# Small triangles in blocks of 32 on four row groups, and head pairs side by side

## The reference, cut to what matters

```python
# FoX: 4 heads of 64; c is the running sum of log_f over the tokens
s = einsum('qd,kd->qk', q, k) * scale + c[q] - c[k]     # causal, softmax, times v
# MoBA: 4 heads, here plain causal attention over 256 keys
# RWKV-7: 8 heads of 64, a recurrence over the 256 tokens
state = state * w + (state @ -kk)[:, None] * (kk * a)[None, :] + v[:, None] * k[None, :]
y = state @ r
```

## Time and profile before

| | before |
|---|---|
| median of 3 runs | 1879.29 us (1876.02 to 1880.2) |
| the profiled execution's own time | 1879.87 us |
| its span, first to last instruction | 1878.6 us |
| PE busy | 1840.2 us, 98% |
| VectorE busy | 1172.0 us, 62% |
| ScalarE busy | 928.5 us, 49% |
| GpSimd busy | 93.6 us, 5% |
| mean granted TensorE clock | 0.990 |
| mixer's part with the change, layer 0 | about 262 to 380 us |
| the same, layer 1 | about 922 to 1037 us |

### The profile page before, as it was taken

How to read it: one execution, slowest core, us unless ns; L and a number is a source line. 1 busy time by engine, 2 the same in 40 slices (tenths; PEclk the granted TensorE clock), 3 DMA queues, 4 the chain that set the end, 5 groups by cost and what they waited for, 6 DMA issues and landing times.

```text
span 1878.6 us, 27992 instructions
## 1 busy us (share of the span) xinstructions
PE 1840.2 (98%) x11596; PEld 1546.9 (82%) x11596; DVE 1172.0 (62%) x1653; ACT 928.5 (49%) x1413; POOL 93.6 (5%) x59
## 2 busy tenths in 40 slices
PE   7999999999999999999999999999999999999999
PEld 6888788878888888887888888888888888888887
DVE  5555577766655565555777666555688548697556
ACT  5444664234544454446642345444555654556553
POOL 0000010040000000000100400000010000000000
PEclk9999998999999999999999999999999999999999
DMA  6755442023455557554420235655554456554454
GB/s 239 249 189 179 168 146 68 25 80 113 158 190 189 191 173 249 191 189 159 156 68 25 80 112 170 207 189 190 167 167 158 156 193 203 168 171 159 159 186 140
DMA packets 83615, 299.18 MB, mean 159 GB/s; under 512 B 9632, under 2 KB 10784, under 8 KB 83232
## 3 DMA queue, kind: packets, MB, share of 16 engines
q1 hardware_dynamic: 79328, 287.87, 46.4%
q10 hardware_dynamic: 3840, 8.03, 1.2%
q0 software_dynamic: 320, 1.48, 0.2%
HBM read 296.30 MB, written 1.05 MB: 158 GB/s over the span
## 4 chain that ended last, share of the span: by engine, by line
PE 94%; DVE 4%; ACT 1%; issue 1%; DMA 0%; POOL 0%; ACTq 0%; DVEq 0%
PE ps L343 24%; PE ps L345 24%; PE ps L344 24%; PE ps L361 2%; PE ps L362 2%; PE ps L363 2%; PE ps L799 1%; PE ps L1194 1%; PE ps L559 1%; PE ps L1197 1%; DVE wlo L325 1%; PE ps L398 1%; PE ps L1185 1%; PE ps L1597 1%; PE ps L771 1%
## 5 line engine op out<-in xcount | busy, mean ns | idle before, releaser
L325 DVE TENSOR_TENSOR wlo<-raw,whi 128x1024 fp32r<-128x1024 f32 (+1 forms) x546 | 662.7, 1222 | 397.2 <-ACT whi L316 395.9
L316 ACT ACTIVATE whi<-raw 128x1024 fp32r<-128x1024 f32 (+1 forms) x546 | 572.1, 1053 | 487.7 <-PE ps L345 460.6
L343 PE MATMUL ps<-whi,a_hi 128*128 128x512 f32 x1696 | 675.4, 398 | 6.7 <-DVE a_lo L1886 1.7
L345 PE MATMUL ps<-whi,a_lo 128*128 128x512 f32 x1696 | 662.3, 390 | 0.0
L344 PE MATMUL ps<-wlo,a_hi 128*128 128x512 f32 x1696 | 661.3, 390 | 0.0
L343 PEld LDWEIGHTS ps<-whi,a_hi 128*128 128x128 f32 x1696 | 319.1, 188 | 76.3 <-DVE a_lo L1886 2.2
L345 PEld LDWEIGHTS ps<-whi,a_lo 128*128 128x128 f32 x1696 | 318.8, 188 | 68.3
L344 PEld LDWEIGHTS ps<-wlo,a_hi 128*128 128x128 f32 x1696 | 319.4, 188 | 62.2
L343 PE MATMUL ps<-whi,h_hi 128*128 128x512 f32 x320 | 124.9, 390 | 0.0
L345 PE MATMUL ps<-whi,h_lo 128*128 128x512 f32 x320 | 124.6, 389 | 0.0
L344 PE MATMUL ps<-wlo,h_hi 128*128 128x512 f32 x320 | 124.5, 389 | 0.0
(11 more groups left out here) (317 smaller groups left out, 1792.9 us busy)
## 6 DMA issues: line engine op xcount, KB each, us to landing
raw<-stream SPq DMA_DIRECT2D x546, 512.0 KB, 3.4
arena<-rows ACTq DMA_DIRECT2D x2, 1026.0 KB, 13.4
arena<-mem ACTq DMA_DIRECT2D x2, 1024.0 KB, 9.7
arena<-lora ACTq DMA_DIRECT2D x2, 768.0 KB, 6.8
arena<-rows ACTq DMA_DIRECT2D x2, 512.0 KB, 4.4
const_tables<-consts POOLq DMA_DIRECT2D x1, 901.0 KB, 4.8
arena<-band POOLq DMA_DIRECT2D x1, 544.0 KB, 4.1
x_res<-x SPq DMA_DIRECT2D x1, 512.0 KB, 3.7
```

The lines of the kernel that those rows point to most:

```text
L316: self.split_hi.mark(act.activation(self.weights(self.whi, u), self.weights(self.raw, u), ACT.Copy), u)
L325: self.split_lo.mark(dve.tensor_tensor(self.weights(self.wlo, u), self.weights(self.raw, u), self.weights(self.whi, u).bitcast(F32), ALU.s ...
L343: pe.matmul(out, a_h, hi, start=start, stop=False, skip_group_check=True)
L345: last = pe.matmul(out, a_l, hi, start=False, stop=True, skip_group_check=True)
```

## The change

Three things change in the mixer of the first block.

1. The triangles are inverted by their diagonal blocks of 32 first. A group now has 4 heads x 4 blocks (`TRIANGLES`: block b on row group b and column group b), 32 x 32 x 32 each, up to level 4; T and its transpose are 32 columns wide per head, both start from PE (`pe_rw_inv0` now makes the triangle and its transpose, 256 records), and VectorE's work has half the columns. The last step (`pe_rw_last`) joins two blocks of 32 to one of 64 with 32 matmuls twice, on two diagonal tiles at a time. ScalarE copies T's blocks to `TI` (`act_rw_last`) and writes half of the joining blocks (`act_rw_last_out`); VectorE writes the other half (`dve_rw_last`).
2. The chunks' products are ordered so that an even and an odd head and the two chunks follow each other, and are marked by pairs of heads instead of heads.
3. FoX's logarithms are summed once, as rows (`pe_at_logs`, copied by `act_at_logs` to `CR`). The scores are made for four heads behind each other, and then one matmul with a single row is added for each head.

```diff
-    for lv in range(6):
+    i, j = s % 32, np.arange(32)[None, :]
+    c["eye32"] = i == j
+    c["pairs"] = np.concatenate([(i // 2 == j // 2) & (i < j), (i // 2 == j // 2) & (i > j)], 1)
+    for lv in range(1, 5):
         b = 1 << lv
         c[f"low{lv}"] = ((i // (2 * b)) == (j // (2 * b))) & ((i // b) % 2 == 1) & ((j // b) % 2 == 0)
-    c["lowT0"] = ((i // 2) == (j // 2)) & (i % 2 == 0) & (j % 2 == 1)
+    c["upper"] = (s // 32) % 2 == 0
...
-        self.T2 = [[t2[:, 512 * (2 * t + g):512 * (2 * t + g + 1)].rearrange("p (a h c) -> p a h c", a=2, h=4)
-                    for g in range(2)] for t in range(NT)]
-        self.XG = [[xn[:, 1024 + 256 * (2 * t + g):1280 + 256 * (2 * t + g)].rearrange("p (h c) -> p h c", h=4)
+
+        self.TC = [t2[:, 512 * t:512 * (t + 1)].rearrange("p (g a h c) -> p g a h c", g=2, a=2, h=4) for t in range(NT)]
+        self.TI = [t2[:, 1024 + 512 * t:1536 + 512 * t].rearrange("p (g h c) -> p g h c", g=2, h=4) for t in range(NT)]
+        self.XG = [[xn[:, 1024 + 128 * (2 * t + g):1152 + 128 * (2 * t + g)].rearrange("p (h c) -> p h c", h=4)
                     for g in range(2)] for t in range(NT)]
...
-        for n in part:
-            h0 = (0, 1, 4, 5)[n]
-            po = HD * (h0 % 2)
+        for pair in range(part[0] // 2, part[-1] // 2 + 1):
             if t:
-                pe.wait_ge(*self.rw_dve("masked", l, 0, n))
+                for n in (2 * pair, 2 * pair + 1):
+                    pe.wait_ge(*self.rw_dve("masked", l, 0, n))
             for i in range(2):
-                for c in range(2):
-                    cols = slice(t * P + c * HD, t * P + (c + 1) * HD)
-                    for a in range(2):
-                        ins = pe.matmul(self.bank(4 + n)[c * HD:(c + 1) * HD, i * 256 + a * P:i * 256 + (a + 1) * P],
-                                        self.BK[po:po + HD, a, h0 // 2 + i, cols],
-                                        self.AR[po:po + HD, 0:2, h0 // 2 + i, cols],
-                                        start=True, stop=True, skip_group_check=True)
-            m.mark(ins, "products", l, t, n)
+                for a in range(2):
+                    for c in range(2):
+                        cols = slice(t * P + c * HD, t * P + (c + 1) * HD)
+                        for odd in range(2):
+                            po = HD * odd
+                            ins = pe.matmul(self.bank(4 + 2 * pair + odd)[c * HD:(c + 1) * HD,
+                                                                          i * 256 + a * P:i * 256 + (a + 1) * P],
+                                            self.BK[po:po + HD, a, 2 * pair + i, cols],
+                                            self.AR[po:po + HD, 0:2, 2 * pair + i, cols],
+                                            start=True, stop=True, skip_group_check=True)
+            m.mark(ins, "products", l, t, pair)
 
     def dve_rw_products(self, l, t, part):
         dve = self.nc.vector
         mask = self.c("mask4").unsqueeze(1).to_broadcast([P, 2, 256])
         for n in part:
...
-        return self.bank(4 + 2 * t + g, 4 * HD).rearrange("p (h c) -> p h c", h=4)
+        return self.bank(4 + 2 * t + g, 128).rearrange("p (h c) -> p h c", h=4)
 
     def t4(self, t, g):
-        return self.bank(4 + 2 * t + g)[:, 4 * HD:8 * HD].rearrange("p (h c) -> p h c", h=4)
-
-    def b4(self, n):
-        return self.c(n).unsqueeze(1).to_broadcast([P, 4, HD])
+        return self.bank(4 + 2 * t + g)[:, 128:256].rearrange("p (h c) -> p h c", h=4)
+
+    def last4(self, t):
+        return self.bank(4 + 2 * t, 256).rearrange("p (g h c) -> p g h c", g=2, h=4)
 
     def pe_rw_inv0(self, l):
+
         pe = self.nc.tensor
         for t, g in self.GROUPS4:
             pe.wait_ge(*self.rw_dve("masked", l, 1, 2 * t + g))
+            A, B = (x[HD * g:HD * (g + 1), 0] for x in (self.AR, self.BK))
             for i in range(4):
-                for c in range(2):
-                    cols = slice(t * P + c * HD, t * P + (c + 1) * HD)
-                    ins = pe.matmul(self.x4(t, g)[c * HD:(c + 1) * HD, i, :], self.AR[HD * g:HD * (g + 1), 0, i, cols],
-                                    self.BK[HD * g:HD * (g + 1), 0, i, cols], start=True, stop=True, skip_group_check=True)
+                for b in range(4):
+                    rows, cols = slice(32 * b, 32 * b + 32), slice(t * P + 32 * b, t * P + 32 * b + 32)
+                    pe.matmul(self.x4(t, g)[rows, i, :], B[:, i, cols], A[:, i, cols], start=True, stop=True,
+                              skip_group_check=True)
+                for b in range(4):
+                    rows, cols = slice(32 * b, 32 * b + 32), slice(t * P + 32 * b, t * P + 32 * b + 32)
+                    ins = pe.matmul(self.t4(t, g)[rows, i, :], A[:, i, cols], B[:, i, cols], start=True, stop=True,
+                                    skip_group_check=True)
             self.rw_pe.mark(ins, "inv0", l, t, g)
 
     def dve_rw_inv0(self, l, groups):
         dve, m = self.nc.vector, self.rw_dve
+        pairs = self.c("pairs").rearrange("p (a c) -> p a c", a=2).unsqueeze(2).to_broadcast([P, 2, 4, 32])
+        eye = self.c("eye32").unsqueeze(1).to_broadcast([P, 8, 32])
         for t, g in groups:
-            T = self.T2[t][g]
...
-            eye = self.c("ident64").unsqueeze(1).to_broadcast([P, 8, HD])
+            ps = self.bank(4 + 2 * t + g, 256).rearrange("p (a h c) -> p a h c", a=2, h=4)
+            m.mark(dve.tensor_tensor(T, ps, pairs, ALU.mult), "pairs", l, t, g)
             T = T.rearrange("p a h c -> p (a h) c")
-            dve.wait_ge(*m("TI 0", l, t, g))
+            dve.wait_ge(*m("pairs", l, t, g))
             m.mark(dve.tensor_tensor(T, T, eye, ALU.add), "T", l, t, g, 0)
 
     def pe_rw_level(self, l, lv):
         pe, m = self.nc.tensor, self.rw_pe
         for t, g in self.GROUPS4:
+            T = self.TC[t][:, g]
             pe.wait_ge(*self.rw_dve("T", l, t, g, lv - 1))
             for i in range(4):
-                for c in range(2):
-                    co = slice(c * HD, (c + 1) * HD)
-                    ins = pe.matmul(self.x4(t, g)[co, i, :], self.MK[co, t, 2 * i + g, 0, :], self.T2[t][g][co, 1, i, :],
+                for rows, cols in self.TRIANGLES:
+                    ins = pe.matmul(self.x4(t, g)[rows, i, :], self.MK[rows, t, 2 * i + g, 0, cols], T[rows, 1, i, :],
                                     start=True, stop=True, skip_group_check=True)
             m.mark(ins, "level x", l, t, g, lv)
         for t, g in self.GROUPS4:
-            T, X = self.T2[t][g], self.XG[t][g]
+            T, X = self.TC[t][:, g], self.XG[t][g]
             pe.wait_ge(*self.rw_dve("X", l, t, g, lv))
             for i in range(4):
-                for c in range(2):
-                    co = slice(c * HD, (c + 1) * HD)
-                    ins = pe.matmul(self.x4(t, g)[co, i, :], X[co, i, :], T[co, 0, i, :], start=True, stop=True,
+                for rows, cols in self.TRIANGLES:
+                    pe.matmul(self.x4(t, g)[rows, i, :], X[rows, i, :], T[rows, 0, i, :], start=True, stop=True,
+                              skip_group_check=True)
+                for rows, cols in self.TRIANGLES:
+                    ins = pe.matmul(self.t4(t, g)[rows, i, :], T[rows, 0, i, :], X[rows, i, :], start=True, stop=True,
                                     skip_group_check=True)
-                    if lv < 5:
-                        ins = pe.matmul(self.t4(t, g)[co, i, :], T[co, 0, i, :], X[co, i, :], start=True, stop=True,
-                                        skip_group_check=True)
             m.mark(ins, "level", l, t, g, lv)
 
     def dve_rw_level(self, l, lv):
         dve, m = self.nc.vector, self.rw_dve
+        low = self.c(f"low{lv}").unsqueeze(1).to_broadcast([P, 4, 32])
         for t, g in self.GROUPS4:
             dve.wait_ge(*self.rw_pe("level x", l, t, g, lv))
-            m.mark(dve.tensor_tensor(self.XG[t][g], self.x4(t, g), self.b4(f"low{lv}"), ALU.mult), "X", l, t, g, lv)
+            m.mark(dve.tensor_tensor(self.XG[t][g], self.x4(t, g), low, ALU.mult), "X", l, t, g, lv)
         for t, g in self.GROUPS4:
-            n = 2 if lv < 5 else 1
-            T = self.T2[t][g][:, 0:n].rearrange("p a h c -> p (a h c)")
+            T = self.TC[t][:, g].rearrange("p a h c -> p (a h c)")
             dve.wait_ge(*self.rw_pe("level", l, t, g, lv))
-            m.mark(dve.tensor_tensor(T, T, self.bank(4 + 2 * t + g, 256 * n), ALU.add), "T", l, t, g, lv)
+            m.mark(dve.tensor_tensor(T, T, self.bank(4 + 2 * t + g, 256), ALU.add), "T", l, t, g, lv)
+
+    def pe_rw_last(self, l):
+
+        pe, m = self.nc.tensor, self.rw_pe
+        for t, g in self.GROUPS4:
+            pe.wait_ge(*self.rw_dve("T", l, t, g, 4))
+            for i in range(4):
+                for up, down in self.HALVES:
+                    ins = pe.matmul(self.x4(t, g)[down, i, :], self.MK[up, t, 2 * i + g, 0, 32:HD],
```

(99 more changed lines are left out.)

4 lines of the change are left out of this document (removed).

## The result

The kernel after takes 1911.03 us (median of 4 runs, 1904.13 to 1912.31) against 1879.04 us of the kernel before on the same chip (4 runs): ratio 1.0166, 95% interval 1.0149 to 1.0184. It is slower by 32 us, where I forecast 29 us less.

The account below looks back on a forecast made before the run. PE was taken as the bound, busy 1840 of 1878.6 us. Triangles 23.6 plus FoX 8.8 less clock 2.4 gave 30.0 us off the profiled 1879.87: 1850 us, with 8 in 10 between 1837 and 1876.

Parts of the forecast that it names:

- Can PE issue a weight load and a matmul each 7.9 ns?: Triangle levels: a burst of nine instructions in at most 20 ns made 7.9 ns a record likely, not certain.
- Rival 1: PE's issue bounds the triangles: no record sooner than 29.2 ns after the last, 1922 us in all; chance 12%.
- Rival 3: Triangle levels run at the lower clock, 8 us a layer and 16 in all, giving 1866 us; chance 12%.
- A record of 32x32: Triangle start and levels to 4: with four tiles, one record ends each 7.9 ns, each tile held 31.6 ns.
- The last step: Last triangle level, two tiles at a time: x and level 1.0 us each, 1.7 us saved a layer.
- my sum of 26.7 + 5: Time a 32x32 record holds its tile: 26.7 ns of streaming and 5 more, 31.6 ns.
- The wait for the masks: PE's wait for VectorE's masks of the products, before the triangles' start: from 1.7 to about 3.5 us.
- FoX: Scores by pairs and logarithms as rows in both layers: saves 8.8 us together.
- the 5.4 forecast: FoX in layer 0: saves 5.4 us, assuming the clock falls again at the second scores and returns earlier.
- forecast 3.4 better: FoX in layer 1, at full clock: scores save 1.4 + 3.45 us, the new logs cost 1.45, so 3.4 saved.
- Clock: Behind the longer wait for the masks: one more half-speed stretch of 3.4 us in both layers together, charged 2.4 us.
- The triangles as a whole: All triangle steps, from products through the last level: save 11.8 us a layer, 23.6 in two.

Follow-up runs that it names:

- the split matmuls: The kernel before, with each matmul of levels 1 to 4 made as two of 32 columns on its 64x64 tile: 1928.52 us, ratio 1.0255.

## Why the prediction was wrong

**The step that failed** is the one under "The triangles" that begins "Can PE issue a weight load and a matmul each 7.9 ns?". The answer was yes, and the question too small. The burst of the earlier trace rows shows nine instructions that were already at hand, and it says nothing of how fast new ones come. I counted a level as 384 records of 7.9 ns, 3.1 us. It is also 768 instructions, three blocks, and at 3.47 us a block at least 10.4 us. From the start of level to level measured 10.7 and 11.9 us for levels 1 to 3 (332.43, 343.09, 354.96), where I had 4.9 and 5.5 and the kernel before 7.0 and 7.3.

**What the kernel before could have told.** A level there is 384 instructions in 7.0 us, 4.7 us a block; in its densest run, x and level without a break, a block is 128 records of 29.2 ns, 3.74 us. It ran just above the supply's 3.47. All my rates were at that edge, so the trace of before could not show the limit, but the count of instructions against packets of q8 was there to be read.

**Rival 1** came nearest, "PE's issue is the bound", 12%, at 1922, against 1911 measured: its threshold (about 15.5 ns a record, 18 with FoX) held, as far as one case can say: the sustained rate is 27, and the change lost. Its mechanism was not right. The limit isn't the time from one record to the next, which went down to 8 ns, but a block of 256; and it lets short stretches pass, as the last level shows. **Rival 3** ("the levels run at the lower clock", 12%) came true as well, beside it: its sign, 0.50 from 333 us on, is there, from 332.10 to 355.99. I had priced it at 16 us for levels that are paced by PE's records; here they are mostly paced by the blocks.

**The other terms.** (1) A record of 32x32 each 7.9 ns forecast, from a tile that is held for 31.6 ns. Both came out at full clock in the first 32 records or so of a row, behind the first four: the starts are 7, 7, 6 and 12 ns apart, so the fourth waits for a tile, and four take 32 ns. The last step, with two tiles at a time, says the same, 64 records in 1.01 us, 15.8 ns each:

```profile
384.82 1.10 PE L1234 MATMUL ps<-arena 32*32 32x32 f32 x58
...
385.83 1.11 PE L1241 MATMUL ps<-arena 32*32 32x32 f32 x59
```

Later in a row the starts alternate, 15 and 2 ns, 8.5 a record; bf16 records come each 8.2 ns at either level of the clock. That is rather PE's own pace of starting a record, but no run separates it. What my sum of 26.7 + 5 doesn't explain is the rest: on 64x64 tiles the weights alone hold the tile as long as 64 columns do, and at the lower clock an fp32 record takes 13.3 ns, 53.3 a tile, which is 2 x 32 columns at 1.2 GHz with nothing on top. (2) The last step: 1.0 us each for x and level forecast, 1.01 and 1.04 measured. (3) The wait for the masks: "3 us or more", 3.1. (4) FoX: 8.8 forecast, 7.9 measured alone. How it divides between the layers one profile can't say, for the clock at the second scores is not the same from one profile to the next. Before, it fell there in layer 0 and not in layer 1, and I built both terms on that. In the profile of FoX's part alone it falls in both layers: layer 0 gave the 5.4 forecast (products at 308.62), layer 1, forecast 3.4 better, was 1.5 worse at its products:

```profile
934.09 2.08 PE L1613 MATMUL ps<-arena 64*128 64x256 f32 x8
936.10 2.08 PE L1617 MATMUL ps<-arena,const_tables 1*128 1x256 f32 x8
938.11 3.68 PE L1021 MATMUL ps<-const_tables,small 128*64 128x128 f32 x32
```

But FoX's change isn't needed for either. Two kernels have FoX's part as before. In the one with the triangles alone the clock does not fall at layer 0's second scores (first two rows, full clock) and the products begin at 306.41, sooner than with FoX's change; in the one with the split matmuls it does fall at layer 1's (last two rows):

```profile
276.39 0.70 PE L1652 MATMUL ps<-arena 64*128 64x256 f32 x2
282.29 1.97 PE L1022 MATMUL ps<-const_tables,small 128*64 128x128 f32 x32
...
967.52 1.22 PE L1598 MATMUL ps<-arena 64*128 64x256 f32 x2
972.97 3.26 PE L1019 MATMUL ps<-const_tables,small 128*64 128x128 f32 x28
```

So that the 5.4 of layer 0 came out is in part luck. Where neither profile has the fall in layer 1 (before, and FoX with the products' order), the way from layer 0's first right-hand side to layer 1's products took 587.5 and 584.3 us, 3.3 less, near the 3.4 forecast. In FoX's part alone 2.6 us came back in the triangles of layer 1, whose low stretch was shorter. (5) Clock, 2.4 forecast: the low stretches grew by 72 us, but mostly inside the levels that wait for instructions anyway. With 37 us of them less and the same instructions the time fell by 2 us, by about 8 at the very most, and blocks come each 3.47 us at either level, so the clock isn't the main cause. (6) The triangles as a whole: 11.8 a layer forecast; with bf16 operands the stage is 11.7 and 10.6 us shorter than before. That agrees, but flatters: half the records went too, and the steps from level to level were 5.6 and 7.4 us, not 4.9 and 5.5. What fp32 would take with instructions always at hand lies, as an estimate from these runs, between 1853 and 1886 (3584 records at 13.3 ns in place of 1792 at 8.2, all of them on PE's path), and no run shows it. So it isn't shown that the triangles would win even then.

Of the miss of 61 us (1850 to 1911), 7 lie between the profiled execution and the median. Of the other 54, 38.5 are the stops of the two layers read from the profile; the rest, some 16, I put down to what runs between stops, at 13.3 ns a record at the lower clock in place of 8, and the GEMM units behind the levels, which start at that clock (0.63 us for a matmul that takes 0.39). How these two divide I haven't separated, nor shown that they are all of it.

**What is best of what was run** with full precision: FoX's part alone, with the products' order, or with the last level by blocks besides, all 1872, 0.3 to 0.6% below the kernel before, with the 64x64 triangles kept.

## What to carry to other kernels

Small matmuls cost instructions before they cost array time: count PE's instructions in a stage (in this case four to an fp32 matmul, two to one with bf16 operands), divide by 256, and hold it against 3.5 us a block; if the planned work of a stage is shorter, the supply is the bound and array packing only adds to it. In a profile the sign is a stop of PE put down to issue at each 256th instruction, and packets of the instruction queue in step with it. A stretch of up to a block behind long matmuls ran free here (256 instructions in the last level, 346 to 506 behind the kernel), so packing can pay there, or where it doesn't raise the count.

## What the runs showed that I had not expected

- PE's instructions come in blocks of 256 (16 KB), one in 3.47 us at best, 13.6 ns an instruction, whether or not other engines transfer. After long matmuls 346 to 506 were ready at once; then each block of fp32 is used up in 1.8 to 2.0 us, one of bf16 in 1.2, and the next is waited for.
- A loop of 128 instructions needs no new blocks: 8 to 9 ns a record, and 0.31 to 0.34 us from one pass to the next.
- With four 32x32 tiles an fp32 record takes 8.0 to 8.5 ns with 32 columns, 13.9 with 64, 27.3 with 128, at full clock, and with two of them 15.8 with 32 columns; with two 64x64 tiles 29.2 to 32.5 ns for 32 or for 64 columns alike.
- At 0.50 of the clock the fp32 records of 32x32 with 32 columns come each 13.3 ns, the bf16 ones each 8.2 as at full clock.
- Whether the clock falls at FoX's second scores differs between profiles of kernels whose work is the same up to there: in layer 0 it fell before and not with the triangles alone.
